# Second attention: VectorE scales each head's first two probability tiles, and the second head's first scores and the exchange stand inside the last value slab

## The chip, the core and the metric

The kernel runs on one core of one Trainium2 chip. Its engines work side by side, each through its own list of instructions, and meet at semaphores: TensorE (PE, matrix products into PSUM), VectorE (DVE), ScalarE (ACT), GpSimd (POOL), and SyncE (SP), which issues the transfers of the weights. The metric is the device time of one execution in microseconds (us), the median of several.

## The reference

Two blocks of two layers each over 512 tokens of width 1024, all in 32-bit floats. The first block has two layers of latent attention, a spatial gate, pooling windows and a gated feed-forward part. The second block has a short-convolution layer and a layer of dilated window attention, each with an MLP and a gated projection behind it. The change is in the dilated attention alone. What is computed there:

```python
q = partial_rotary(qkv[:, :, 0], positions)      # 3 groups x 8 heads of 128
k = partial_rotary(qkv[:, :, 1], positions)
v = qkv[:, :, 2]
for g, (window, dilation) in enumerate(((128, 1), (512, 4), (2048, 16))):
    s = einsum(q, k) * 128 ** -0.5               # band of at most 128 keys back
    lse = logsumexp(s)
    probs = exp(s - lse)
    o_g, lse_g = probs @ v, lse
weights = softmax(stack(lses), axis=0)           # over the three groups
o = sum(weights * outs)                          # one output per head
```

For one head this is one softmax over all three groups' scores, so each probability tile is multiplied in the end by one factor per row (the reciprocal of the mass of all groups).

## The kernel before

**The stages.** All weights come as a stream of slabs of 128 x 2048 numbers. SyncE loads a slab into one of two places, GpSimd splits it into a high and a low part (w_high, L449, by tensor_scalar, and w_low, L454, by tensor_tensor, four pieces each), and TensorE multiplies three times per block (L568 to L570: high by high, low by high, high by low) with the activations, which are split alike. A slab takes TensorE 48 matmuls. The heavy loops are all of this kind.

**The second attention** (`attn` on each engine) runs in two batches of four heads. A batch is twelve slabs for queries and keys, six for values (`for g in range(GROUPS): for half in range(2)`), then the four heads, with one more slab behind the first batch and the output projection of four slabs behind the second. Ahead of the last value slab, (g, half) = (2, 1), TensorE makes all scores of the batch's first head H0. A value slab's second half ends in four quarters, c = 0 to 3, one PSUM bank (4 + c) each, and ScalarE evicts each quarter to v_tok (L1495), which counts drained[4 + c].

**A head** has eight score tiles, 0 to 7 (128x256 each, tile 4 is 128x128), in four pairs, one PSUM bank a pair. Tiles 0 to 3 hold the dilated groups, 4 to 7 the near one. In steps, with the names of the code:

- `scores(H, k)`, TensorE: pair k (L979 for pairs 0 and 1, L985 for 2 and 3).
- `mask_tile(H, n)`, VectorE, L2003: adds the mask, writes the tile to `probs`, and takes the row's extreme. `exponential(H, n)`, ScalarE, L1465: the exponential in place, with the row's sum.
- `send(H, set_)`, VectorE, L2010: lays out these statistics. `exchange(H)`, TensorE, L996: moves them between rows, since the groups order their tokens differently, into a free corner of PSUM bank 2.
- `difference(H)` and `make_factors(H)`, VectorE, L2017 to L2027, with ScalarE's `stats_exponential(H)`, L1470, between them: the factors of the head, `factors_made`.
- `scale_head(H)`, GpSimd, L522: all eight tiles times their factors, in order, `tile_scaled` counted for each.
- `turn_pair(H, k)`, TensorE, L1008: transposes pair k of the scaled tiles, when they are scaled. `copy_turned(H, k)`: the transposed pair to SBUF, pairs 0 and 2 by ScalarE (L1477), 1 and 3 by VectorE (L2034).
- `values_pair(H, k)`, TensorE, L1026: product with the values. `copy_out(H)`, VectorE, L2039: the head's output.

Everything is in the order in which it is written, engine by engine; there is no scheduler. TensorE interleaves two heads: scores of H + 1 between the transposes and values of H, and the last two value pairs of H - 1 before scores pair 2 of H + 1. In the fourth head of a batch, the slab behind the batch fills the time until the factors. GpSimd does between the scalings, in the first batch, pieces of the split of the slab that comes two later (`pieces`, L504 and L511), and in the second batch the split of finished heads' outputs (`split_head`, L529 and L531), and behind the eighth head all pieces of the output projection's second slab. The outputs of heads 6 and 7 are split by ScalarE (L1254) and VectorE (L2088).

Of the kernel before, what the change touches and what calls it, by code (L numbers as in the profile page):

```python
# [175 lines left out]
def build(nc, a):  # L176

    ctx = ExitStack()
    with ctx:
# [3 lines left out]
        def sem(name):  # L183
            return ctx.enter_context(nc.semaphore(name))
# [164 lines left out]
        tile_scaled = sem("tile_scaled")  # L349
        pair_turned = sem("pair_turned")  # L350
# [90 lines left out]
        def _(pool):  # L441
# [73 lines left out]
            def scale_head(H):  # L515

                pool.wait_ge(factors_made, H + 1)
                for n in range(TILES):
                    at, w = tile_columns(n)
                    a, set_ = tile_slot(n)  # L520
                    tile = probs[:, H % 2, at:at + w]
                    pool.tensor_scalar(tile, tile, fac[:, H % 2, 3, a, set_:set_ + 1], None, ALU.mult).then_inc(tile_scaled, 1)  # L522
# [42 lines left out]
        def _(pe):  # L565
# [433 lines left out]
            def turn_pair(H, k):  # L999

                pe.wait_ge(tile_scaled, TILES * H + 2 * k + 2)
                if k >= 2:
                    pe.wait_ge(pair_copied[k - 2], H + 1)
                else:
                    at_least(pe, pair_copied[k + 2], H)
                for n in range((PAIR_AT[k + 1] - PAIR_AT[k]) // P):
                    at = PAIR_AT[k] + n * P
                    last = pe.transpose(ps[:, 4 + k % 2, n * P:(n + 1) * P], probs[:, H % 2, at:at + P], ident[:])  # L1008
                last.then_inc(pair_turned, 1)
# [21 lines left out]
            def attn(p):  # L1031
# [27 lines left out]
                for batch in range(2):  # L1059
# [18 lines left out]
                    for g in range(GROUPS):  # L1078
                        for half in range(2):
# [8 lines left out]
                            for c in range(TOK):  # L1088
                                if half == 0:
# [18 lines left out]
                    for b in range(4, 8):  # L1108
                        if b >= 6:
                            pe.wait_ge(drained[b], p.drain[b] + used[b])  # L1110
                    for j in range(BATCH_HEADS):
                        H = H0 + j
                        if j < BATCH_HEADS - 1:
                            scores(H + 1, 0)
                            exchange(H)
# [10 lines left out]
                            turn_pair(H, 1)  # L1126
                            values_pair(H, 0)
# [50 lines left out]
        def _(act):  # L1178
# [272 lines left out]
            def attn(p):  # L1451
# [27 lines left out]
                for batch in range(2):  # L1479
# [4 lines left out]
                    for g in range(GROUPS):  # L1484
# [3 lines left out]
                        for c in range(TOK):  # L1488
                            act.wait_ge(*((tile_done, t0 + 3 * g + c + 1) if c < 3 else (slab_done, s0 + 2 * g + 2)))
# [6 lines left out]
                    for j in range(BATCH_HEADS):  # L1496
                        H = H0 + j
                        stats_exponential(H)
# [51 lines left out]
        def _(dve):  # L1550
# [408 lines left out]
            def attn(p):  # L1959
# [60 lines left out]
                def make_factors(H):  # L2020
# [6 lines left out]
                    dve.reciprocal(fac[:, H % 2, 3], mass).then_inc(factors_made, 1)  # L2027

# [237 lines left out]
```

## Time and profile before

| what | value |
|---|---|
| median of 3 runs | 2636.18 us (2635.54 to 2640.35) |
| profiled execution | 2643.82 us, span 2641.8 us |
| TensorE (PE) busy | 2571.2 us, 97% of the span |
| GpSimd (POOL) busy | 1824.0 us, 69% |
| VectorE (DVE) busy | 1081.3 us, 41% |
| ScalarE (ACT) busy | 472.8 us, 18% |
| granted TensorE clock, mean | 0.987 |
| scaling of tiles, L522, 64 of them | 55.5 us |

The profiled execution has a span, from its first to its last instruction, and a time, which also holds what lies around it (2.0 us here). "Busy" is the sum of an engine's instructions. A row of the order of time shows the start, the time and the number of like instructions in a row, and in brackets how long the engine had idled before it and what ended that. TensorE's matmuls overlap, so a matmul of 0.40 us may be followed by the next after 0.23 us. The two batches' heads run from about 1889 to 1922 us and from about 2130 to 2165 us.

### The profile page before, as it was taken

To read this page: it belongs to the slowest core of one execution; us is meant where nothing else is said; L and a number is where in the kernel's file an instruction comes from. 1 tells how busy PE (TensorE), PEld (TensorE's weight loads), DVE (VectorE), ACT (ScalarE), POOL (GpSimd) and SP (SyncE) were. 2 spreads that over 40 slices of the span, in tenths; PEclk is the share of its full clock that TensorE was granted. 3 is DMA by queue.
4 is the path that set the end of the run, shared out by engine and by line. 5 is a ranking of instruction groups with operands and counts; after the bars stand their busy time and mean duration, and the time that the engine had idled before them with its cause. 6 is when DMAs were issued, how large, how long until landed. Compare 5 with 4: busy or idle time off the path is not lost.

```text
span 2641.8 us, 31829 instructions
## 1 busy us (share of the span) xinstructions
PE 2571.2 (97%) x11758; PEld 2133.6 (81%) x11758; DVE 1081.3 (41%) x1706; ACT 472.8 (18%) x886; POOL 1824.0 (69%) x1837
## 2 busy tenths in 40 slices
PE   7989999999899999999999999999999989999997
PEld 6768888888688888888888888888888978888885
DVE  4763332036633330344530422795378244504225
ACT  3432111023421110200200102300300032100022
POOL 5537777665267777677786776787677777867763
PEclk9999999999999999999999999999999999999998
DMA  4112222231122222222322222222112203222221
GB/s 155 49 48 95 96 95 96 95 118 49 38 106 95 95 95 96 96 96 96 104 96 96 95 97 98 97 96 97 63 64 95 99 30 104 96 96 96 96 97 63
DMA packets 36895, 236.46 MB, mean 90 GB/s; under 512 B 4048, under 2 KB 5584, under 8 KB 9168
## 3 DMA queue, kind: packets, MB, share of 16 engines
q1 hardware_dynamic: 33456, 230.78, 25.2%
q10 hardware_dynamic: 3360, 4.57, 0.6%
q8 instruction: 56, 0.92, 0.1%
q14 instruction: 23, 0.19, 0.0%
HBM read 233.24 MB, written 2.10 MB: 89 GB/s over the span
## 4 chain that ended last, share of the span: by engine, by line
PE 92%; DVE 3%; POOL 2%; issue 2%; ACT 1%; DMA 0%; DVEq 0%; SPq 0%; POOLq 0%; ACTq 0%
PE psum L568 29%; PE psum L569 29%; PE psum L570 29%; POOL probs L522 2%; PE psum L788 1%; PE psum L902 1%; POOL w_low L454 1%; PE psum L918 0%; PE psum L598 0%; DMA x_res<-in_x 0%; PE psum L1026 0%; PE psum L934 0%; PE psum L615 0%; POOL w_high L449 0%; PE psum L862 0%
## 5 line engine op out<-in xcount | busy, mean ns | idle before, releaser
L454 POOL TENSOR_TENSOR w_low<-w_stage,w_high 128x512 fp32r<-128x512 f32 x856 | 1145.4, 1370 | 17.9
L449 POOL TENSOR_SCALAR w_high<-w_stage 128x512 fp32r<-128x512 f32 x856 | 567.3, 690 | 731.8 <-PE psum L570 720.3
L568 PE MATMUL psum<-x_high,w_high 128*128 128x512 f32 x1664 | 655.7, 394 | 15.9 <-DVE x_low L1581 15.0
L569 PE MATMUL psum<-x_low,w_high 128*128 128x512 f32 x1664 | 649.4, 390 | 0.0
L570 PE MATMUL psum<-x_high,w_low 128*128 128x512 f32 x1664 | 649.0, 390 | 0.0
L568 PEld LDWEIGHTS psum<-x_high,w_high 128*128 128x128 f32 x1664 | 313.4, 188 | 84.3 <-issue 17.4
L569 PEld LDWEIGHTS psum<-x_low,w_high 128*128 128x128 f32 x1664 | 313.5, 188 | 67.3 <-issue 2.4
L570 PEld LDWEIGHTS psum<-x_high,w_low 128*128 128x128 f32 x1664 | 313.4, 188 | 65.4
L1618 DVE TENSOR_TENSOR psum<-psum,x_res 128x512 f32<-128x512 f32 x64 | 44.8, 700 | 465.4 <-PE psum L570 462.5
L568 PE MATMUL psum<-mlp_high,w_high 128*128 (+1 forms) x576 | 224.1, 389 | 0.0
L569 PE MATMUL psum<-mlp_low,w_high 128*128 (+1 forms) x576 | 224.1, 389 | 0.0
L570 PE MATMUL psum<-mlp_high,w_low 128*128 (+1 forms) x576 | 224.1, 389 | 0.0
L568 PE MATMUL psum<-attn_x_high,w_high 128*128 128x512 f32 x384 | 150.1, 391 | 0.0
L570 PE MATMUL psum<-attn_x_high,w_low 128*128 128x512 f32 x384 | 149.4, 389 | 0.0
L569 PE MATMUL psum<-attn_x_low,w_high 128*128 128x512 f32 x384 | 149.4, 389 | 0.0
L568 PE MATMUL psum<-ffn_high,w_high 128*128 (+1 forms) x352 | 136.9, 389 | 0.0
L569 PE MATMUL psum<-ffn_low,w_high 128*128 (+1 forms) x352 | 136.9, 389 | 0.0
L570 PE MATMUL psum<-ffn_high,w_low 128*128 (+1 forms) x352 | 136.9, 389 | 0.0
L1233 ACT ACTIVATE x_res<-psum 128x512 f32<-128x512 f32 x72 | 43.2, 600 | 493.9 <-DVE psum L1618 487.9
L568 PEld LDWEIGHTS psum<-mlp_high,w_high 128*128 128x128 f32 x576 | 108.1, 188 | 22.6
L570 PEld LDWEIGHTS psum<-mlp_high,w_low 128*128 128x128 f32 x576 | 108.1, 188 | 22.4
L569 PEld LDWEIGHTS psum<-mlp_low,w_high 128*128 128x128 f32 x576 | 108.1, 188 | 22.3
(289 smaller groups left out, 3399.8 us busy)
## 6 DMA issues: line engine op xcount, KB each, us to landing
w_stage<-in_wstream SPq DMA_DIRECT2D x216, 1024.0 KB, 4.9
x_res<-in_x SPq DMA_DIRECT2D x2, 1024.0 KB, 11.8
out_x<-attn_out SPq DMA_DIRECT2D x8, 256.0 KB, 2.1
inv_count_sb<-in_inv_count ACTq DMA_DIRECT2D x2, 512.0 KB, 8.8
ple_proj<-in_p ACTq DMA_DIRECT2D x2, 512.0 KB, 3.6
w_spat<-in_spatial ACTq DMA_DIRECT2D x2, 256.0 KB, 5.2
diag_sb<-in_diag ACTq DMA_DIRECT2D x2, 256.0 KB, 9.4
qk<-in_mask ACTq DMA_DIRECT2D x1, 306.0 KB, 2.9
```

Source lines behind the costliest of these rows:

```text
L449: last = pool.tensor_scalar(wh[:, s, part], stage[:, s, part], 1.0, 1.0, ALU.mult, ALU.mult)
L454: last = pool.tensor_tensor(wl[:, s, part], stage[:, s, part], wh[:, s, part].bitcast(F32), ALU.subtract)
L522: pool.tensor_scalar(tile, tile, fac[:, H % 2, 3, a, set_:set_ + 1], None, ALU.mult).then_inc(tile_scaled, 1)
L568: pe.matmul(out, wa, ra, start=start, stop=False)
L569: pe.matmul(out, wa, rb, start=False, stop=False)
L570: return pe.matmul(out, wb, ra, start=False, stop=stop)
L788: last = pe.matmul(ps[:, 6, at + c:at + c + 1], W[rows, n % 2, c * P:(c + 1) * P], ones[rows, 0:1], start=True, stop=True)
L902: last = pe.matmul(ps[:, h % 2, kb * P:], vt1[:, kb, h * V_HEAD:(h + 1) * V_HEAD], pt1[:, kb, kb * P:], start=kb == 0, stop=kb == TOK - 1)
L1233: act.activation(x[:, m, :], ps[:, m, :], ACT.Copy)
L1618: tt(ps[:, m, :], ps[:, m, :], x[:, m, :], ALU.add).then_inc(x_summed, 1)
```

## The change

Three things are edited, in this attention alone.

1. VectorE scales tiles 0 and 1 of each head, in `make_factors`, right behind the factors, and counts `front_scaled`. GpSimd's `scale_head` starts at tile 2. `turn_pair(H, 0)` waits for `front_scaled`, the others for `tile_scaled` with six tiles a head.
2. TensorE makes scores pair 0 of the batch's second head and the exchange of the first head ahead of quarter c = 3 of the last value slab, and no more behind the slab. On ScalarE, `stats_exponential(H0)` stands ahead of the eviction of that quarter.
3. The wait for the evictions of banks 6 and 7 (`drained`) goes from behind the slab to the place ahead of `values_pair(H0, 0)`.

```diff
             def scale_head(H):
                 pool.wait_ge(factors_made, H + 1)
-                for n in range(TILES):
+                for n in range(2, TILES):
...
             def turn_pair(H, k):
-                pe.wait_ge(tile_scaled, TILES * H + 2 * k + 2)
+                if k == 0:
+                    pe.wait_ge(front_scaled, 2 * (H + 1))
+                else:
+                    pe.wait_ge(tile_scaled, (TILES - 2) * H + 2 * k)
...
                             for c in range(TOK):
+                                if (g, half, c) == (2, 1, 3):
+                                    scores(H0 + 1, 0)
+                                    exchange(H0)
...
-                    for b in range(4, 8):
-                        if b >= 6:
-                            pe.wait_ge(drained[b], p.drain[b] + used[b])
                     for j in range(BATCH_HEADS):
                         H = H0 + j
                         if j < BATCH_HEADS - 1:
-                            scores(H + 1, 0)
-                            exchange(H)
+                            if j:
+                                scores(H + 1, 0)
+                                exchange(H)
                             scores(H + 1, 1)
...
                             turn_pair(H, 1)
+                            if j == 0:
+                                for b in (6, 7):
+                                    pe.wait_ge(drained[b], p.drain[b] + used[b])
                             values_pair(H, 0)
...
                         for c in range(TOK):
+                            if (g, c) == (2, 3):
+                                stats_exponential(H0)
...
-                        stats_exponential(H)
+                        if j:
+                            stats_exponential(H)
...
                     dve.reciprocal(fac[:, H % 2, 3], mass).then_inc(factors_made, 1)
+                    dve.wait_ge(factors_made, H + 1)
+                    for n in range(2):
+                        tile = probs[:, H % 2, 2 * P * n:2 * P * (n + 1)]
+                        dve.tensor_scalar(tile, tile, fac[:, H % 2, 3, n, 0:1], None, ALU.mult).then_inc(front_scaled, 1)
```

TensorE at the end of the first batch's last value slab, before. The slab's last matmuls stand ahead; L979 and L985 are scores of the second head, L996 the exchange, L1008 the first head's transposes.

```order
L570 MATMUL psum<-w_high,attn_x_low 128x512
L979 MATMUL psum<-qk 128x128 [waits tile_masked,drained7,drained6]
L979 MATMUL psum<-qk 128x128 x3
L996 MATMUL psum<-sent_stats,turn 64x16 [waits stats_sent]
L996 MATMUL psum<-sent_stats,turn 64x16 x3
L979 MATMUL psum<-qk 128x128 [waits tile_masked]
L979 MATMUL psum<-qk 128x128 x3
L985 MATMUL psum<-qk 128x128 [waits stats_used,tile_masked]
L985 MATMUL psum<-qk 128x256
L1008 MATMUL psum<-ident,probs 128x128 [waits tile_scaled,drained5,drained4]
```

The same place in the changed kernel (L980, L986, L997 and L1012 are L979, L985, L996 and L1008 of before; between the exchange and the next scores stand the last quarter's twelve matmuls, of which the first and the last are shown).

```order
L571 MATMUL psum<-w_high,attn_x_low 128x512
L980 MATMUL psum<-qk 128x128 [waits tile_masked]
L980 MATMUL psum<-qk 128x128 x3
L997 MATMUL psum<-sent_stats,turn 64x16 [waits stats_sent]
L997 MATMUL psum<-sent_stats,turn 64x16 x3
L569 MATMUL psum<-w_high,attn_x_high 128x512
...
L571 MATMUL psum<-w_high,attn_x_low 128x512
L980 MATMUL psum<-qk 128x128 [waits tile_masked]
...
L986 MATMUL psum<-qk 128x128 [waits stats_used,tile_masked]
L986 MATMUL psum<-qk 128x256
L1012 MATMUL psum<-ident,probs 128x128 [waits front_scaled,drained5,drained4]
```

Scores pair 0 and the exchange now stand 12 matmuls ahead of the slab's end and wait for no eviction; the first transpose waits for VectorE's count in place of GpSimd's.

VectorE from the first head's difference to the second head's next masks, before (L2017 to L2027 make the factors, ISA L2003 is a mask):

```order
L2017 TENSOR_TENSOR factors<-own_stats,psum 128x8 [waits stats_turned]
L2018 TENSOR_SCALAR factors<-factors 128x8 [waits dve_step]
L2003 ISA probs,own_stats<-psum,mask 128x256
L2003 ISA own_stats 128x1
L2024 TENSOR_TENSOR factors<-factors,psum 128x8 [waits stats_exp]
L2026 TENSOR_TENSOR factors<-factors,own_stats 128x8 [waits stats_used]
L2027 RECIPROCAL factors<-factors 128x8 [waits dve_step]
L2003 ISA probs,own_stats<-psum,mask 128x256 [waits pair_scored]
```

And in the changed kernel (L2028 to L2038 make the factors, ISA L2014 is a mask):

```order
L2028 TENSOR_TENSOR factors<-own_stats,psum 128x8 [waits stats_turned]
L2029 TENSOR_SCALAR factors<-factors 128x8 [waits dve_step]
L2014 ISA probs,own_stats<-psum,mask 128x256
L2014 ISA own_stats 128x1
L2035 TENSOR_TENSOR factors<-factors,psum 128x8 [waits stats_exp]
L2037 TENSOR_TENSOR factors<-factors,own_stats 128x8 [waits stats_used]
L2038 RECIPROCAL factors<-factors 128x8 [waits dve_step]
L2042 TENSOR_SCALAR probs<-probs,factors 128x256 [waits factors_made]
L2042 TENSOR_SCALAR probs<-probs,factors 128x256
L2014 ISA probs,own_stats<-psum,mask 128x256 [waits pair_scored]
```

Two scalings stand ahead of the masks of tiles 2 and 3, in every head.

## Rows read from the trace of the kernel before

**Rows 1.** The page: busy time of the engines; chain that ended last, by line.

```profile
PE 2571.2 (97%) x11758; PEld 2133.6 (81%) x11758; DVE 1081.3 (41%) x1706; ACT 472.8 (18%) x886; POOL 1824.0 (69%) x1837
...
PE psum L568 29%; PE psum L569 29%; PE psum L570 29%; POOL probs L522 2%; PE psum L788 1%; PE psum L902 1%; POOL w_low L454 1%; PE psum L918 0%; PE psum L598 0%; DMA x_res<-in_x 0%; PE psum L1026 0%; PE psum L934 0%; PE psum L615 0%; POOL w_high L449 0%; PE psum L862 0%
```

**Rows 2.** Windows: stretch, length, busy us (instructions) of PE, PEld, DVE, ACT, POOL, clock, DMA.

```profile
1885.00:1922.50 37.50, 33.08 (x253) 28.47 (x252) 17.72 (x77) 17.04 (x59) 28.10 (x32) 1.00 0.02 8
2126.00:2165.50 39.50, 33.41 (x255) 28.76 (x254) 18.91 (x77) 17.06 (x59) 30.15 (x34) 1.00 0.03 10
2177.00:2185.00 8.00, 6.75 (x29) 4.95 (x29) 5.19 (x6) 2.40 (x5) 7.92 (x8) 1.00 0.00 0
```

**Rows 3.** Order of time, GpSimd: start, us, what, [idle before, what ended it].

```profile
1891.94 6.92 POOL L522 TENSOR_SCALAR probs<-probs,factors 128x256 f32<-128x256 f32 x8 [10.63 <-DVE factors L2027]
...
1902.21 6.95 POOL L522 TENSOR_SCALAR probs<-probs,factors 128x256 f32<-128x256 f32 x8 [1.01 <-DVE factors L2027]
...
2133.20 6.92 POOL L522 TENSOR_SCALAR probs<-probs,factors 128x256 f32<-128x256 f32 x8 [10.62 <-DVE factors L2027]
...
2144.38 6.96 POOL L522 TENSOR_SCALAR probs<-probs,factors 128x256 f32<-128x256 f32 x8 [0.36 <-DVE factors L2027]
```

**Rows 4.** Waits of 1885 to 1922.5, then 2126 to 2186: us, times, longest.

```profile
PE psum L1008 <- POOL probs L522: 3.4, 7, 1.5
...
PE psum L1008 <- POOL probs L522: 5.0, 8, 1.6
```

**Rows 5.** Order of time, TensorE, first batch's heads.

```profile
1889.05 1.13 PE L979 MATMUL psum<-qk 128*128 128x128 f32 x8 [0.82 <-issue]
...
1893.92 0.63 PE L1008 MATMUL psum<-ident,probs 128*128 128x128 f32 x4 [1.48 <-POOL probs L522]
...
1900.39 0.42 PE L996 MATMUL psum<-sent_stats,turn 128*64 128x16 f32 x8
...
1904.10 0.66 PE L1008 MATMUL psum<-ident,probs 128*128 128x128 f32 x4
...
1905.90 0.66 PE L1008 MATMUL psum<-ident,probs 128*128 128x128 f32 x4 [0.28 <-POOL probs L522]
...
1909.22 0.66 PE L1008 MATMUL psum<-ident,probs 128*128 128x128 f32 x4 [0.38 <-POOL probs L522]
```

**Rows 6.** Order of time, ScalarE's last evictions of the value slab; VectorE's reciprocal.

```profile
1885.45 0.69 ACT L1495 ACTIVATE v_tok_wide<-psum,stat 128x512 f32<-128x512 f32 x1 [2.13 <-PE psum L570]
1888.27 0.69 ACT L1495 ACTIVATE v_tok_wide<-psum,stat 128x512 f32<-128x512 f32 x1 [2.13 <-PE psum L570]
...
1891.63 0.20 DVE L2027 RECIPROCAL factors<-factors 128x8 f32<-128x8 f32 x1
```

**Rows 7.** Order of time, first block: VectorE's tile scaling twice, GpSimd's split.

```profile
147.33 0.35 DVE L1943 TENSOR_SCALAR work<-work,stat 128x256 f32<-128x256 f32 x1
...
133.10 1.28 DVE L1943 TENSOR_SCALAR work<-work,stat 128x256 f32<-128x256 f32 x1 [0.24 <-DVE stat L1942]
...
130.51 5.00 POOL L454 TENSOR_TENSOR w_low<-w_stage,w_high 128x512 fp32r<-128x512 f32 x4
```

**Rows 8.** Order of time, VectorE, factors of the second batch's second head.

```profile
2143.15 0.89 DVE L2026 TENSOR_TENSOR factors<-factors,own_stats 128x8 f32<-128x8 f32 x1
```

**Rows 9.** Order of time behind the last head: GpSimd, VectorE, TensorE.

```profile
2178.24 5.79 POOL L511 TENSOR_TENSOR w_low<-w_stage,w_high 128x512 fp32r<-128x512 f32 x4
...
2177.74 2.65 DVE L2088 TENSOR_TENSOR attn_low<-attn_out,attn_high 128x512 fp32r<-128x512 f32 x2
...
2178.74 0.50 PE L568 MATMUL psum<-attn_high,w_high 128*128 128x512 f32 x1 [0.26 <-DVE attn_low L2088]
...
2184.13 0.47 PE L568 MATMUL psum<-attn_high,w_high 128*128 128x512 f32 x1 [0.98 <-issue]
```

**Rows 10.** Order of time, TensorE, from the first head's scores to the slab.

```profile
1876.59 0.60 PE L568 MATMUL psum<-w_high,attn_x_high 128*128 128x512 f32 x1
1877.02 0.40 PE L569 MATMUL psum<-w_low,attn_x_high 128*128 128x512 f32 x1
```

More of the change, by code:

```diff
@@ L349, in build @@
         tile_scaled = sem("tile_scaled")
+        front_scaled = sem("front_scaled")
         pair_turned = sem("pair_turned")
```

## The prediction

> **What bounds the kernel now.** I read the page first, then the busy time in three stretches, then GpSimd's scalings in order of time, then what TensorE waits for. On the page TensorE is busy 97% of the span, and its three product lines make 87% of the chain. The only other line above 1% there is GpSimd's scaling of probability tiles, L522, with 2%, some 53 us [rows 1]; eight heads at 6.9 us [rows 3] are 55 us, so every one of the eight scalings is on the chain. A gain has to come out of the few stretches where TensorE idles. In the first batch of four heads it is busy 33.08 of 37.50 us (4.42 idle), in the second 33.41 of 39.50 (6.09 idle), in the 8 us after the last head 6.75 of 8.00 (1.25 idle), all at a granted clock of 1.00 [rows 2]. Together that is 11.8 us, and no edit of this stage can give more.
>
> GpSimd's rows show a loop: it scales eight tiles, idles until the next factors, and scales again; in the first batch the period is 1902.21 - 1891.94 = 10.27 us [rows 3]. The waits say how much of it TensorE feels: the transposes of L1008 waited for L522 3.4 us in the first batch and 5.0 in the second [rows 4]. The other idle time is 0.82 us ahead of the first scores behind the value slab, at 1889.05, and the same in the second batch (two in all) [rows 5]: they wait for drained 6 and 7, and ScalarE's last eviction runs from 1888.27 to 1888.96 [rows 6]. Last, TensorE waits 0.98 us at 2184.13 for the low part of an output slab, which GpSimd finished at 2178.24 + 5.79 = 2184.03 [rows 9].
>
> **The change, part by part.** (a) *Scores pair 0 of the second head and the exchange go ahead of the last quarter of the value slab.* No work is added; the wait for drained 6 and 7 moves behind turn_pair(H, 1). Before, from the first score (1889.05) to the reciprocal's end (1891.63 + 0.20) it took 2.78 us [rows 5, 6]. After, scores and exchange take about 1.4 us of TensorE, then come the slab's last 12 matmuls, 2.8 us by the distance of ScalarE's last two evictions (1885.45 to 1888.27) [rows 6], then pairs 1 and 2 of the scores, about 2 us. The factors are made halfway through those 12 matmuls, so the first transpose comes some 3.4 us behind them, and two tiles need 2 x 0.87 = 1.7 us even on GpSimd (6.92 for eight) [rows 3]. So 2 x 0.82 us goes, and so does the largest wait for L522, 1.48 us at 1893.92 [rows 5], with its like in the second batch. Quarter 3's eviction now has two score pairs and two transposes ahead of its reader, over 3 us, and takes 0.69 [rows 6]. The exponential of the factors stands ahead of that eviction on ScalarE; it would hold it up only if the exchange were late, and the statistics that are exchanged come from scores made ahead of this slab.
>
> Price: TensorE switches once more between the four-byte matmuls and the slab's. After the first head's scores the slab's first matmul was followed after 1877.02 - 1876.59 = 0.43 us [rows 10], where 2.82 / 12 = 0.235 is the rule. I take 0.2 us for each batch, 0.4; bounds 0 (it merges with the switch behind the slab) and 0.8 (twice as much).
>
> (b) *Tiles 0 and 1 on VectorE, six on GpSimd.* GpSimd's scaling shrinks by 1.7 to about 5.2 us, and its loop to 10.27 - 1.7 = 8.6 us. TensorE's own work in a period is 10.27 less the waits of 0.28 at 1905.90 and 0.38 at 1909.22 [rows 5]: 9.6 us. The loop is then TensorE's, with 1.0 us to spare on GpSimd, and all of [rows 4], 3.4 + 5.0 = 8.4 us, can go.
>
> What do the two tiles cost on VectorE? The nearest row is L1943, the same form (128x256, SBUF to SBUF, a factor per partition): 0.35 us at 147.33 with GpSimd idle, 1.28 us at 133.10, within GpSimd's tensor_tensor of 130.51 to 135.51 [rows 7]. Both engines start on the same factors, GpSimd 0.11 us after the reciprocal (1891.83 to 1891.94) [rows 3, 6]; VectorE, which waits for its own result, should be no later. So the first tile likely gets through at once and the second may wait for one GpSimd tile. Bounds for both: 0.7 and 2.6 us; I take 1.6. What of it does TensorE see? The exchange of head 1 ended at 1900.39 + 0.42 = 1900.81, its first transpose started at 1904.10, 3.3 us later [rows 5]. The factors are there about 1.3 us after the exchange (GpSimd's start at 1902.21 less 0.1), so the front tiles at 2.9: hidden, with 0.4 us to spare. At 2.6 us they would be 0.6 us late. Behind the two tiles on VectorE stand the masks of tiles 2 and 3, the copy of the head before and the masks of 4 and 5, and behind those ScalarE's exponentials; VectorE idled there, since masks 6 and 7 come only with scores pair 3. At 1.6 us they stay covered, barely.
>
> (c) *GpSimd against VectorE in the second batch.* There GpSimd also splits two heads' outputs between scalings: 2144.38 - 0.36 - 2140.12 = 3.9 us [rows 3]. VectorE's L2026, a step of 8 elements like the reciprocal at 0.20, took 0.89 beside it [rows 6, 8], and the loop is some 11 us. After, GpSimd needs 5.2 + 3.9 = 9.1 us for a head and TensorE 9.6. In the second head GpSimd is free before the factors, for the first head lasts longer; in the third its split can still run into them. I leave 0.4 us of waiting there (bounds 0 and 2).
>
> The Trainium skill has a rule for this place ("SBUF — State Buffer", section Who interferes with whom): a VectorE `tensor_scalar` between SBUF operands can enter a 2-port mode, it and a GpSimd instruction then exclude each other whole, and issue order decides who blocks. The rows at 0.35 and 1.28 agree. By that rule the second tile waits a whole GpSimd tile in every head, the 1.6 us; without it both would take 0.7. The sum is the same by either, since both are hidden.
>
> (d) *The tail.* GpSimd reaches the late slab 1.7 us sooner, less some 0.3 for standing behind VectorE; that covers the 0.98 us. What is late next: the low part of head 6's output, for which TensorE already waits 0.26 us at 2178.74. VectorE starts it at 2177.74 [rows 9], and GpSimd, earlier by then, will be at tensor_tensor pieces of 1.25 us (four in 5.00) [rows 7], which can block it for longer. I take 0.3 us more (bounds 0 and 0.9).
>
> **Sum.** Removed: 8.4 + 2 x 0.82 + 0.98 = 11.0 us. Added: 0.4 + 0.4 + 0.3 = 1.1. Net 9.9 us, off the profiled span of 2641.8 (to 2631.9) and off that execution's time of 2643.82 alike. That execution is 7.6 us above the median of the runs; I take the stage to be the same in both and subtract from the median: 2636.18 - 9.9 = 2626.3. What stands behind the stage moves forward as a block, since TensorE sets its pace [rows 1].
>
> **Rivals.**
> *A partial gain.* Both front tiles are blocked (2.6 us), and in the second batch the factor steps before them too. The first transpose of heads 1 and 2 of each batch is then 0.6 to 1.0 us late. For it: 0.89 and 1.28 us where GpSimd was busy [rows 7, 8]. Against: GpSimd starts from idle. Price 4 x 0.8 = 3.2 us: gain 6.7, 2629.5.
> *No change.* VectorE and ScalarE close a loop as long as GpSimd's was: the masks of 2 and 3 behind the front tiles delay the exponentials, the copy of the first transpose and the next exchange, and the periods stay 10.3 and 11. Only the first heads and the tail gain, 2 x (0.82 + 1.5) + 0.98 - 1.1 = 4.5 us: 2631.7.
> *Slower.* One mechanism, at L2042 on VectorE: its two tiles take turns with GpSimd's so badly that the first transpose comes later than now. From that transpose to the end of the next exchange TensorE needs 9.6 - 3.3 = 6.3 us, so a period exceeds today's mean of 10.6 once the front tiles are ready over 4.3 us after the exchange, at 1.5 us for each tile; to eat the other 4.5 us as well, the four middle periods must each lose 1.1 us, at 2.05 us for each. That is two GpSimd tiles for each of VectorE's, and no row shows it. At 2.8 us for each, the loss is 4 x 2.6 - 4.5 = 5.9 us: 2642.1.
>
> **Chances.** Forecast 0.72, partial gain 0.16, no change 0.09, slower 0.03. A measurement of this kernel can tell 0.2%, 5.3 us, from no change; two thirds of the partial case lie above that. Faster by over 0.2%: 0.83; within: 0.14; slower: 0.03. Range: from 2623.0 (all 11.8 us, and 1.4 for the scatter of the runs, which spread over 4.8) to 2631.5 (the partial case, and part of no change).
>
> **What would show it.** Right, if in the new trace the transposes have no wait for GpSimd, heads follow each other in 9.6 to 9.8 us in both batches, GpSimd's scaling takes 5.2 to 5.5 us and starts inside the value slab for the first head, and nothing waits at the second output slab. VectorE's tiles at 0.35 and about 1.2 us would confirm (b); two of over 1.2 with a wait of TensorE on them are the partial case. A wait for copies of transposed tiles at a period of 10.3 is the third. Wrong altogether, if the granted clock falls in the stage, or if time goes outside 1885 to 2185 us.

## The result, and the profile after

| | before | after |
|---|---|---|
| median of 6 runs each | 2636.42 us (2635.54 to 2640.35) | 2623.05 us (2617.34 to 2629.31) |
| ratio, with its 95% interval | | 0.9944, 0.9933 to 0.9955 |
| profiled execution, span | 2643.82, 2641.8 us | 2629.31, 2627.4 us |
| mean granted clock of that execution | 0.987 | 0.987 |

The change gains 14.8 us by the ratio and 14.5 between the two profiled executions. The two medians differ by 13.4. The forecast was 9.9, below the 11.9 to 17.7 us of the interval. Of the 2636.18 us from which it subtracted, the ratio leaves 2621.4 us, which lies below the range of 2623.0 to 2631.5 (the bare median of 2623.05 stands on its edge). The direction was right and the size was not.

The lines of the kernel after are numbered a little higher: L980 and L986 are scores, L997 the exchange, L1012 transposes, L1030 values, L523 GpSimd's scaling, L2042 VectorE's two tiles, L2038 the reciprocal, L569 to L571 the products. First the page of after, with the lines that answer to [rows 1]:

```profile
PE 2567.9 (98%) x11758; PEld 2135.2 (81%) x11758; DVE 1085.6 (41%) x1722; ACT 471.8 (18%) x886; POOL 1808.0 (69%) x1821
...
PE 96%; DVE 2%; ACT 1%; issue 1%; POOL 0%; DMA 0%; DVEq 0%; SPq 0%; POOLq 0%; ACTq 0%
```

GpSimd's scaling was 2% of the chain before; GpSimd as a whole is 0% of it now. Look also at TensorE's sum: 2571.2 us before, 2567.9 after, for the same 11758 matmuls, in two executions of the same mean clock. TensorE's instructions were not changed, only their order, so a sum that becomes 3.3 us shorter is where the surplus shows first. Next the windows of after, the two batches and the first 8 us of the tail (columns as in [rows 2]):

```profile
1885.00:1922.50 37.50, 37.31 (x280) 34.03 (x279) 21.93 (x91) 16.92 (x60) 26.81 (x31) 1.00 0.12 45
2117.00:2155.00 38.00, 37.76 (x280) 34.90 (x280) 22.29 (x91) 17.38 (x61) 26.36 (x30) 1.00 0.08 29
2165.00:2173.00 8.00, 8.00 (x35) 6.20 (x34) 4.32 (x5) 3.36 (x6) 7.39 (x8) 1.00 0.25 75
```

TensorE idles 0.2 us a batch where it idled 4.4 and 6.1 [rows 2], at the same clock of 1.00. Now the order of time, TensorE, first batch of after: the scores and the exchange inside the slab, the slab's end, and then one head, to be held against [rows 5]:

```profile
1886.04 1.05 PE L980 MATMUL psum<-qk 128*128 128x128 f32 x8
1887.02 0.42 PE L997 MATMUL psum<-sent_stats,turn 128*64 128x16 f32 x8
1887.37 0.62 PE L569 MATMUL psum<-w_high,attn_x_high 128*128 128x512 f32 x1
1887.83 0.40 PE L570 MATMUL psum<-w_low,attn_x_high 128*128 128x512 f32 x1
...
1890.18 0.40 PE L571 MATMUL psum<-w_high,attn_x_low 128*128 128x512 f32 x1
1890.41 1.05 PE L980 MATMUL psum<-qk 128*128 128x128 f32 x8
...
1891.96 0.60 PE L1012 MATMUL psum<-ident,probs 128*128 128x128 f32 x4
...
1896.83 1.06 PE L980 MATMUL psum<-qk 128*128 128x128 f32 x8
...
1905.85 0.50 PE L980 MATMUL psum<-qk 128*128 128x128 f32 x3
```

No bracket is left. GpSimd (answers to [rows 3]), second head of the first batch and second and third of the second:

```profile
1899.63 5.26 POOL L523 TENSOR_SCALAR probs<-probs,factors 128x256 f32<-128x256 f32 x6 [3.18 <-DVE factors L2038]
...
2134.83 5.25 POOL L523 TENSOR_SCALAR probs<-probs,factors 128x256 f32<-128x256 f32 x6 [1.65 <-DVE factors L2038]
...
2144.38 5.30 POOL L523 TENSOR_SCALAR probs<-probs,factors 128x256 f32<-128x256 f32 x6 [0.37 <-DVE factors L2038]
```

GpSimd waits for the factors now and nobody waits for it. VectorE, the factors and the two tiles of two of these heads (answers to [rows 6] and [rows 8]):

```profile
1899.33 0.20 DVE L2038 RECIPROCAL factors<-factors 128x8 f32<-128x8 f32 x1
1899.57 0.84 DVE L2042 TENSOR_SCALAR probs<-probs,factors 128x256 f32<-128x256 f32 x2
...
2143.34 0.69 DVE L2037 TENSOR_TENSOR factors<-factors,own_stats 128x8 f32<-128x8 f32 x1
2144.07 0.20 DVE L2038 RECIPROCAL factors<-factors 128x8 f32<-128x8 f32 x1
2144.31 0.84 DVE L2042 TENSOR_SCALAR probs<-probs,factors 128x256 f32<-128x256 f32 x2
```

Both tiles together take 0.84 us. L2037 took 0.69 us in the second of these heads, where it takes 0.17 in the others. Last the tail, GpSimd, VectorE and TensorE at the second output slab (answers to [rows 9]):

```profile
2163.70 5.99 POOL L512 TENSOR_TENSOR w_low<-w_stage,w_high 128x512 fp32r<-128x512 f32 x4
...
2164.91 2.38 DVE L2103 TENSOR_TENSOR attn_low<-attn_out,attn_high 128x512 fp32r<-128x512 f32 x2
...
2169.86 0.39 PE L569 MATMUL psum<-attn_high,w_high 128*128 128x512 f32 x1
```

**Where the 14.4 us of the span went.** A column of idle time hides something here, so I count from start to start of TensorE's own rows. The stations of a batch are the first head's last scores, the scores pair 0 of heads 2, 3 and 4, and the fourth head's exchange. In the kernel after, the first row counts the slab without the scores and the exchange inside it, (1886.04 - 1876.05) + (1890.41 - 1887.37) = 13.03. The 1.33 us of those, 1887.37 - 1886.04, count with the head behind.

| stretch | first batch, before, after | gain | second batch, before, after | gain |
|---|---|---|---|---|
| value slab, to the scores behind it | 13.80, 13.03 | 0.77 | 13.80, 13.03 | 0.77 |
| to scores pair 0 of head 3 | 10.36, 7.75 | 2.61 | 10.36, 7.74 | 2.62 |
| to scores pair 0 of head 4 | 10.30, 9.02 | 1.28 | 11.21, 9.02 | 2.19 |
| to the exchange of head 4 | 12.46, 11.06 | 1.40 | 13.24, 11.21 | 2.03 |
| sum | 46.92, 40.86 | 6.06 | 48.61, 41.00 | 7.61 |

From the first matmul of the first output slab to the first of the second: 18.66 and 17.26, a gain of 1.40. All else, unchanged code: 0.8 us lost ahead of the first batch and 0.13 gained behind the tail. 6.06 + 7.61 + 1.40 + 0.13 - 0.8 = 14.4.

**The theories.** The head is what I went for: 10.30 us with 0.66 us of idle time [rows 5], and 9.02 after, with none.
A: a wait of TensorE costs more than the idle time that the trace shows at it, since a wait also breaks the overlap of neighbouring matmuls, and that part is booked as busy.
B: the surplus is the granted clock (runs of one kernel spread over some 10 us).
C: TensorE's own work in a head is 9.6 us as predicted, and the surplus was gained by something else, such as the move inside the slab.

### The profile page after: what moved, and what is told of

It is laid out like the page before. It is cut to its first block, busy times and chain, and to the rows that moved or that the text cites. A ratio compares the mean times of both kernels' runs of the same rounds, so it can differ in the third digit from the quotient of the medians.

```text
span 2627.4 us, 31829 instructions
## 1 busy us (share of the span) xinstructions
PE 2567.9 (98%) x11758; PEld 2135.2 (81%) x11758; DVE 1085.6 (41%) x1722; ACT 471.8 (18%) x886; POOL 1808.0 (69%) x1821
## 4 chain that ended last, share of the span: by engine, by line
PE 96%; DVE 2%; ACT 1%; issue 1%; POOL 0%; DMA 0%; DVEq 0%; SPq 0%; POOLq 0%; ACTq 0%
PE psum L569 30%; PE psum L570 30%; PE psum L571 30%; PE psum L1030 1%; PE psum L789 1%; PE psum L903 1%; PE psum L980 1%; PE psum L919 0%; PE psum L986 0%; PE psum L1012 0%; PE psum L599 0%; DMA x_res<-in_x 0%; PE psum L616 0%; PE psum L935 0%; PE psum L863 0%
## 5 line engine op out<-in xcount | busy, mean ns | idle before, releaser
L569 PE MATMUL psum<-x_high,w_high 128*128 128x512 f32 x1664 | 655.9, 394 | 15.6 <-DVE x_low L1592 15.0
L571 PE MATMUL psum<-x_high,w_low 128*128 128x512 f32 x1664 | 649.3, 390 | 0.0
L569 PEld LDWEIGHTS psum<-x_high,w_high 128*128 128x128 f32 x1664 | 313.7, 189 | 83.8 <-issue 17.4
L571 PEld LDWEIGHTS psum<-x_high,w_low 128*128 128x128 f32 x1664 | 313.5, 188 | 65.6
L569 PE MATMUL psum<-mlp_high,w_high 128*128 (+1 forms) x576 | 224.1, 389 | 0.0
L571 PE MATMUL psum<-mlp_high,w_low 128*128 (+1 forms) x576 | 224.1, 389 | 0.0
L569 PE MATMUL psum<-attn_x_high,w_high 128*128 128x512 f32 x384 | 150.1, 391 | 0.0
L571 PE MATMUL psum<-attn_x_high,w_low 128*128 128x512 f32 x384 | 149.4, 389 | 0.0
L569 PE MATMUL psum<-ffn_high,w_high 128*128 (+1 forms) x352 | 136.9, 389 | 0.0
L571 PE MATMUL psum<-ffn_high,w_low 128*128 (+1 forms) x352 | 136.9, 389 | 0.0
L571 PEld LDWEIGHTS psum<-mlp_high,w_low 128*128 128x128 f32 x576 | 108.1, 188 | 22.6
L569 PEld LDWEIGHTS psum<-mlp_high,w_high 128*128 128x128 f32 x576 | 108.1, 188 | 22.3
```

The lines of the kernel that those rows point to most:

```text
L569: pe.matmul(out, wa, ra, start=start, stop=False)
L571: return pe.matmul(out, wb, ra, start=False, stop=stop)
```

## The experiments

All runs below have their own runs of the kernel before beside them: 20, median 2637.47 us, for the first four; 10, median 2638.31, for the last four. "Stretch" means the sum rows of the table, first and second batch, and "period" scores pair 0 of head 3 to that of head 4. Diffs are against the changed kernel.

### The changed kernel once more

No edit.

> The changed kernel once more, unaltered, for the size of the gain and the granted clock of each run. In the two profiles the stretch from the first head's L985 scores to the slab behind the four heads went from 47.27 to 41.20 us (first batch) and from 48.96 to 41.35 (second), and the tail to the second output slab from 18.66 to 17.26: 6.07 + 7.61 + 1.40 = 15.1 us. Theory A (the surplus over the forecast 9.9 lies in waits that the idle column shows too small): the stretches repeat within 0.2 us, and the ratio is 0.9943 to 0.9950 (15.1 to 13.2 us). Theory B (part of the surplus is the clock, granted higher in the runs of the changed kernel): the ratio comes back to 0.996 with equal clocks, 10 us.

Measured: 2622.68 us median of 5, ratio 0.9944 (0.9929 to 0.9959). Stretches 40.86 and 41.55 us, period 9.02. The ratio and the first batch repeat to the last digit. The second batch is 0.55 us longer than in the first profile, outside the 0.2 us that was expected. Its rows show why: one of the steps that make the factors, eight numbers per row and 0.17 us long elsewhere, ran beside a piece of GpSimd's split and ended with it (order of time, VectorE and GpSimd).

```profile
2140.32 1.29 DVE L2029 TENSOR_SCALAR factors<-factors 128x8 f32<-128x8 f32 x1
...
2140.32 1.27 POOL L532 TENSOR_TENSOR attn_low<-attn_out,attn_high 128x512 fp32r<-128x512 f32 x1
```

### The scaling alone

The move is undone: scores pair 0 and the exchange stand behind the slab again, the wait for the evictions ahead of them, and `stats_exponential(H0)` on ScalarE at its old place (not shown).

```diff
                             for c in range(TOK):
-                                if (g, half, c) == (2, 1, 3):
-                                    scores(H0 + 1, 0)
-                                    exchange(H0)
...
+                    for b in (6, 7):
+                        pe.wait_ge(drained[b], p.drain[b] + used[b])
                     for j in range(BATCH_HEADS):
                         H = H0 + j
                         if j < BATCH_HEADS - 1:
-                            if j:
-                                scores(H + 1, 0)
-                                exchange(H)
+                            scores(H + 1, 0)
+                            exchange(H)
```

> VectorE scales tiles 0 and 1, but scores and exchange stay behind the value slab, as before. Theory A: heads 1 and 2 have the period of 9.02 us of the changed kernel in both batches; the first head keeps the 0.82 us wait for the eviction and a short wait for the front tiles (factors + 0.84 us against the end of scores pair 2, about 0.3 us), so each batch loses 1.3 to 1.6 us against the changed kernel: stretches of 42.6 and 42.8 us, 2.8 us in all, gain about 12 us. Theory C (TensorE's own work is 9.6 us a head, as the idle column has it, and the rest comes with the earlier exchange and the copies behind it): period 9.6, gain 9 us.

Measured: 2626.22 us median of 10, ratio 0.9960 (0.9948 to 0.9972). Stretches 42.57 and 43.53. The windows of one period in each batch:

```profile
1897.91:1906.93 9.02, 9.02 (x79) 8.46 (x78) 6.55 (x28) 5.23 (x19) 8.01 (x11) 1.00 0.00 1
2134.82:2144.32 9.50, 9.40 (x79) 8.44 (x78) 7.40 (x28) 5.00 (x19) 8.97 (x11) 1.00 0.01 2
```

The period of the first batch is 9.02 without the move, so TensorE's own work in a head is at most 9.0 us, and C, as far as it puts the surplus down to the move, falls. (That it did not come from the early front tiles is for the padded runs below.) The second batch missed the expectation: a stretch of 43.53 where 42.8 was expected, and a period of 9.50. There GpSimd has almost no time to spare. From one scaling to the next it takes 2148.03 - 2138.52 = 9.51 us, as long as the period: 5.2 for six tiles, 3.9 for two outputs, and 0.37 until the factors. The factors are late because a step of theirs is held up by the last piece of GpSimd's own split, and ends with it, as in the run before (order of time, VectorE and GpSimd):

```profile
2137.30 0.88 DVE L2029 TENSOR_TENSOR factors<-factors,own_stats 128x8 f32<-128x8 f32 x1
...
2136.89 1.27 POOL L532 TENSOR_TENSOR attn_low<-attn_out,attn_high 128x512 fp32r<-128x512 f32 x1
```

The idle column shows 0.10 of the 0.48 us; the weight loads (PEld) waited 0.21, 0.23 and 0.29 us in that period, for VectorE's tiles, ScalarE's copy and GpSimd. The order of time, TensorE, shows what the move is for:

```profile
1889.22 1.13 PE L980 MATMUL psum<-qk 128*128 128x128 f32 x8 [0.82 <-issue]
...
1893.02 0.63 PE L1012 MATMUL psum<-ident,probs 128*128 128x128 f32 x4 [0.41 <-DVE probs L2034]
```

Without it the first head's first transposes wait for VectorE's tiles.

### The move alone

GpSimd scales all eight tiles again, VectorE none.

```diff
-                for n in range(2, TILES):
+                for n in range(TILES):
...
-                    for n in range(2):
-                        tile = probs[:, H % 2, 2 * P * n:2 * P * (n + 1)]
-                        dve.tensor_scalar(tile, tile, fac[:, H % 2, 3, n, 0:1], None, ALU.mult).then_inc(front_scaled, 1)
```

> Scores and exchange move into the value slab, GpSimd scales all eight tiles, as before. Theory A: GpSimd closes the loop again, periods of heads 1 and 2 at 10.3 and 11.2 us as before, tail as before (18.7), while the first head gains all its four waits with their hidden part, 3.4 us a batch: stretches 43.9 and 45.6, gain 6.8 us in all. By the idle column alone the first head would gain 0.82 + 1.48 + 0.22 + 0.36 - 0.2 = 2.7 us a batch, 5.4 in all.

Measured: 2629.69 us median of 9, ratio 0.9967 (0.9955 to 0.9978). Stretches 43.22 and 44.65, shorter than theory A expected by 0.7 and 0.95 us; the second batch's period is 10.86, not 11.2. The windows of one period, then TensorE in the first of them:

```profile
1895.78:1906.07 10.29, 9.63 (x79) 8.34 (x78) 6.05 (x26) 5.22 (x19) 9.04 (x12) 1.00 0.00 1
2133.41:2144.27 10.86, 9.65 (x79) 8.33 (x78) 6.53 (x26) 5.23 (x19) 10.41 (x12) 1.00 0.01 2
```

```profile
1902.27 0.66 PE L1009 MATMUL psum<-ident,probs 128*128 128x128 f32 x4 [0.28 <-POOL probs L523]
...
1905.58 0.66 PE L1009 MATMUL psum<-ident,probs 128*128 128x128 f32 x4 [0.38 <-POOL probs L523]
```

With the old scaling the first batch's period, its 9.63 us of busy time and both waits are those of before. The halves overlap: in the first batch the scaling alone gains 4.35 us, the move alone 3.70, and both 6.06, not 8.05. The 2.0 us that both claim lie in the first head, up to the scores pair 0 of head 3: there the scaling alone gains 1.67 us, the move alone 2.91, and both 2.61. Its largest wait for scaled tiles is 1.48 us by its bracket in [rows 5].

### The scaling made long again, first try

Everything as changed, but GpSimd multiplies two tiles by 1.0 ahead of its six, so that it should be late as before while VectorE still has its two tiles.

```diff
                 pool.wait_ge(factors_made, H + 1)
+                for n in (6, 7):
+                    at, w = tile_columns(n)
+                    tile = probs[:, H % 2, at:at + w]
+                    pool.tensor_scalar(tile, tile, 1.0, 1.0, ALU.mult, ALU.mult).then_inc(padded, 1)
                 for n in range(2, TILES):
+                    if n == 6:
+                        pool.wait_ge(padded, 2 * (H + 1))
...
```

> The changed kernel with two more GpSimd instructions (tiles 6 and 7 times 1.0) ahead of its six scalings, so that VectorE still makes the front tiles early, while GpSimd's part takes 7.0 us as before. Theory A (each wait of a transpose costs its idle time and an exposed weight load and pipeline start): the period goes back to 10.3 us in the first batch and 11.2 in the second, with only 0.3 to 0.4 us of idle time shown at the second and fourth transpose; gain as with the move alone, 6.8 us. Theory C (the surplus of 0.6 us a head came from the early front tiles): period 9.7 and 10.6.

Measured: 2623.41 us median of 4, ratio 0.9946 (0.9928 to 0.9964). Stretches 41.46 and 42.62, period 9.39. I had mis-sized the pad: the two took 0.96 us, not 1.85, since a tile times two immediate numbers takes 0.5 us where one times a factor per row takes 0.92. So neither theory's figure for the period (10.3 and 9.7) applies. Still, the period grew by 0.37 us and TensorE's rows show a wait of 0.15.

### The same with a longer pad

Four tiles, 4 to 7, instead of two.

> As the padded kernel before it, but with four idle GpSimd instructions (tiles 4 to 7 times 1.0): two took 0.96 us there, not the 1.85 wanted. GpSimd's part of a head is then 1.92 + 5.1 = 7.0 us, as in the kernel before, with the front tiles on VectorE. Theory A (a wait of a transpose costs its idle time and some 0.2 us of exposed weight load and pipeline start): periods back to 10.2 to 10.4 us in the first batch and 11.0 to 11.3 in the second, the stretch from the first head's L985 scores to the fourth exchange 43.2 to 43.6 us in the first batch (40.86 in the changed kernel) and 44.5 to 45.2 in the second, while the idle column shows no more than 0.7 us a head. Theory C (the early front tiles give the surplus): periods 9.7 and 10.6.

Measured: 2627.78 us median of 5, ratio 0.9962 (0.9949 to 0.9976). Stretches 42.56 and 44.59, periods 9.91 and 11.04. GpSimd and TensorE in the first batch, order of time, and the window of that period:

```profile
1898.55 1.47 POOL L523 TENSOR_SCALAR probs<-probs 128x128 f32<-128x128 f32 x4 [1.42 <-DVE factors L2045]
1900.00 5.12 POOL L530 TENSOR_SCALAR probs<-probs,factors 128x256 f32<-128x256 f32 x6
```

```profile
1905.18 0.66 PE L1019 MATMUL psum<-ident,probs 128*128 128x128 f32 x4 [0.36 <-POOL probs L530]
```

```profile
1895.76:1905.67 9.91, 9.43 (x79) 8.42 (x78) 6.93 (x28) 5.23 (x19) 8.49 (x14) 1.00 0.01 2
```

The pad was short again (1.47 us; pad and six tiles are 6.59, eight tiles were 6.92), and the first batch fell short of what A expected: a period of 9.91 for 10.2 to 10.4, a stretch of 42.56 for 43.2 to 43.6. The second batch's 11.04 and 44.59 lie in A's ranges. By its size alone the first batch's period, between C's 9.7 and A's 10.2, would decide nothing. The comparison inside the period does not depend on the pad's length: it grew by 9.91 - 9.02 = 0.89 us, of which TensorE's idle time is 0.48 and its "busy" time 9.43 - 9.02 = 0.41; by C it would have grown by the idle time alone. VectorE, which the pad could have held up, did not cost it: its two tiles took 0.89 us, and the first transposes came 1900.31 - 1899.65 = 0.66 us behind their scores, as in after. That is A, on its own.

### GpSimd held until VectorE's tiles are done

```diff
             def scale_head(H):

-                pool.wait_ge(factors_made, H + 1)
+                pool.wait_ge(front_scaled, 2 * (H + 1))
```

> GpSimd's scale_head waits for front_scaled in place of factors_made, so that it starts when VectorE has done its two tiles. If the two engines exclude each other, VectorE's pair takes 0.6 us (2 x 0.27 to 0.35, pipelined) in place of 0.84; if its 0.84 us is VectorE's own time, it stays 0.84. GpSimd starts 0.5 to 0.8 us later after the factors; with 1.0 to 1.3 us to spare in the first batch the stretch there stays at 40.9 us within 0.2; in the second batch, where GpSimd has no slack, up to 1 us more.

Measured, a single run, so no gain is read from its time: 2619.09 us at a mean clock of 0.991. Stretches 41.18 and 41.81, periods 9.34 and 9.20. The first batch is 0.08 us outside what was expected. VectorE's two tiles, GpSimd held:

```profile
1896.90 0.62 DVE L2042 TENSOR_SCALAR probs<-probs,factors 128x256 f32<-128x256 f32 x2
```

0.62 us against 0.84 with GpSimd at work, and GpSimd's six take 5.10 instead of 5.26. So the two engines do get in each other's way here, for 0.22 us a head on VectorE. Avoiding it starts GpSimd some 0.7 us later, and the first batch's period is 0.3 us longer. TensorE does not wait for GpSimd there but for VectorE's copy of the second pair (L2049, 0.24 us by its bracket): the `send` ahead of that copy took 0.51 us in this period, where after has 0.19.

### The wait for the evictions ahead of the scores again

The move stays; only its third part is undone.

```diff
+                    for b in (6, 7):
+                        pe.wait_ge(drained[b], p.drain[b] + used[b])
                     for j in range(BATCH_HEADS):
...
-                            if j == 0:
-                                for b in (6, 7):
-                                    pe.wait_ge(drained[b], p.drain[b] + used[b])
                             values_pair(H, 0)
```

> The changed kernel with the wait for drained 6 and 7 back behind the value slab, ahead of scores pair 1 of the second head. TensorE then waits for ScalarE's eviction of the last quarter, 0.8 us of idle time as before, and by theory A 0.2 us that the idle column does not show: both stretches 1.0 us longer (41.9 and 42.0 to 42.5), 2 us in all. By the idle column alone 0.8 us each.

Measured: 2624.31 us median of 4, ratio 0.9951 (0.9936 to 0.9966). Stretches 42.04 and 42.39, periods 9.03 and 9.02. TensorE at the slab's end:

```profile
1883.06 0.40 PE L571 MATMUL psum<-w_high,attn_x_low 128*128 128x512 f32 x1
1884.29 1.13 PE L980 MATMUL psum<-qk 128*128 128x128 f32 x8 [0.82 <-issue]
```

From start to start 1.23 us, where after has 1890.41 - 1890.18 = 0.23. The wait costs 1.00 us at its place, and its bracket says 0.82; the first batch's stretch is 1.18 us longer than with the wait moved. This is the second time that an added wait costs more than its idle time, at another line and with another releaser. (The remaining 0.18 us of the 1.18 lies behind this place.)

### The copy of the second pair ahead of the statistics

The changed kernel still has short waits of the weight loads for VectorE's copies. In the waits of 1885 to 1918 us of after:

```profile
PEld psum L1030 <- DVE probs_t L2049: 0.9, 4, 0.3
```

This version copies the second pair first, and spreads GpSimd's splits of the second batch otherwise.

```diff
-                        for h in ((0, 1), (2, 3), (4,), (5,))[j]:
+                        for h in ((0, 1), (2,), (3, 4), (5,))[j]:
...
-                            send(H + 1, 0)
                             copy_turned(H, 1)
+                            send(H + 1, 0)
```

> A try at a faster version: VectorE copies the second transposed pair ahead of its send (in the changed kernel TensorE's weight loads of L1030 wait 0.15 to 0.3 us a head for that copy), and GpSimd splits one output less before the third head of the second batch, where its split runs into VectorE's factors (0.16 and 0.55 us of wait in two profiles), and one more behind it. First-batch stretch 40.86 less 0.1 to 0.5 us, second batch 41.0 to 41.5 down to 40.6; 0.5 to 1.2 us in all, less than the time of a run can tell, so the ratio stays at 0.994 to 0.9945. The rival: the send comes later, the exchange of the next head with it, and nothing is gained.

Measured: 2621.72 us median of 5, ratio 0.9938 (0.9924 to 0.9951). Stretches 40.34 and 40.45 us, periods 8.92 in both. The stretches are the shortest of all, 0.52 and 0.55 below after. The first batch has the copy's edit alone, so its 0.52 us is the copy's; in the second batch the two edits are not separated. It also shows that the 9.02 us of after still held 0.1 us of waiting. In the time of a whole execution, 1 us is less than these runs can tell from the changed kernel (0.9933 to 0.9955).

## Why the prediction was right in direction and wrong in size

**The failed step** is one assumption with two faces: "TensorE's own work in a period is 10.27 less the waits of 0.28 [...] and 0.38 [...]: 9.6 us", and "Together that is 11.8 us, and no edit of this stage can give more". Both take the idle column for the whole cost of a wait. TensorE's own work in a period is at most 9.02 us, and the stage gave 15.07 us in its two stretches and the tail. The term of the sum that this mis-sized is the waits for GpSimd: 8.4 - 0.4 = 8.0 us predicted, 12.1 measured. Here is what the column leaves out. TensorE and its weight loads (PEld) in one head of after, order of time:

```profile
1900.72 0.82 PE L986 MATMUL psum<-qk 128*128 128x128 f32 x4
1901.38 0.60 PE L1012 MATMUL psum<-ident,probs 128*128 128x128 f32 x4
1901.81 1.03 PE L986 MATMUL psum<-qk 128*128 128x256 f32 x4
1902.68 0.60 PE L1012 MATMUL psum<-ident,probs 128*128 128x128 f32 x4
```

```profile
1901.16 0.57 PEld L1012 LDWEIGHTS psum<-ident,probs 128*128 128x128 f32 x4
...
1902.46 0.57 PEld L1012 LDWEIGHTS psum<-ident,probs 128*128 128x128 f32 x4
```

The same places before, where the transposes had to wait (their own rows are 1904.10 and 1905.90 in [rows 5]):

```profile
1903.30 0.82 PE L985 MATMUL psum<-qk 128*128 128x128 f32 x4
...
1904.59 1.03 PE L985 MATMUL psum<-qk 128*128 128x256 f32 x4
```

```profile
1904.10 0.42 PEld L1008 LDWEIGHTS psum<-ident,probs 128*128 128x128 f32 x4 [0.38 <-POOL probs L522]
...
1905.90 0.42 PEld L1008 LDWEIGHTS psum<-ident,probs 128*128 128x128 f32 x4 [0.68 <-POOL probs L522]
```

After, a transpose's weights are loaded 0.22 us ahead of it (1901.16, 1901.38) and it starts while the scores' modelled end still runs (1900.72 + 0.82 = 1901.54). Before, load and transpose start together. The tile that is waited for is the stationary operand, so its load does not go ahead; and the idle column begins to count only where the scores' modelled end runs out. The first transposes stood at 1904.10 with no bracket on PE at all, yet came 0.80 us behind their scores instead of 0.66; PEld's row tells it, 0.38. By start to start:

| from, to | before | after | more | shown idle |
|---|---|---|---|---|
| scores pair 2, first transposes | 0.80 | 0.66 | 0.14 | none |
| scores pair 3, second transposes | 1.31 | 0.87 | 0.44 | 0.28 |
| values pair 0, third transposes | 1.00 | 0.89 | 0.11 | none |
| values pair 1, fourth transposes | 1.43 | 1.00 | 0.43 | 0.38 |
| inside the four groups of transposes | 1.87 | 1.71 | 0.16 | none |

Together 1.28 us, and 0.66 shown. The windows of the same period say it in one line each, first before (1899.41, 2140.67), then after:

```profile
1899.41:1909.71 10.30, 9.64 (x80) 8.34 (x78) 6.05 (x26) 5.22 (x19) 9.29 (x13) 1.00 0.00 1
2140.67:2151.88 11.21, 9.67 (x79) 8.34 (x78) 6.71 (x26) 5.23 (x19) 10.68 (x13) 1.00 0.01 1
```

```profile
1896.83:1905.85 9.02, 9.02 (x80) 8.47 (x79) 6.55 (x28) 5.22 (x19) 6.22 (x7) 1.00 0.00 1
2132.02:2141.04 9.02, 9.02 (x79) 8.46 (x78) 6.55 (x28) 5.22 (x19) 7.29 (x9) 1.00 0.01 2
```

The same 79 or 80 matmuls are 9.64 us "busy" with waits between them and 9.02 without. A good part of this could have been had before the change. PEld's waits for GpSimd stand beside PE's, 4.6 us against 3.4 in the first batch and 6.1 against 5.0 in the second; that is 2.3 us more, and still less than what came. And in the eighth head of before, where nothing waits for GpSimd, the fourth transposes follow values pair 1 after 2174.55 - 2173.66 = 0.89 us, against 1.43 with a shown wait of 0.38.

**Theory B falls** by comparing runs at the same mean clock, in us:

| clock | before | after, again |
|---|---|---|
| 0.987 | 2643.6 (3 runs, median) | 2629.3 (the profiled one of after) |
| 0.989 | 2637.8 (median) | 2621.8 to 2622.8 |
| 0.990 | 2633.9 to 2635.8 | 2621.2 |

The gain is 14.3 us in the first line, 15.0 to 16.0 in the second and 12.7 to 14.6 in the third, so above 9.9 in each. The clock is given to 0.001, and a step of that is 2.6 us of 2630, so this says no more than that. The clock in the stage is 1.00 in every window; what spreads the runs lies ahead of it (the stage's first station stood at 1875.25, 1876.05 and 1873.69 us in before, after and after again, and at 1864.35 in the single run with GpSimd held, at 0.991). The surplus is in the two stretches and the tail, at a clock of 1.00.

**The terms one by one.**

- (a) *The move.* Predicted 2 x 0.82 less 2 x 0.2; measured 2 x 0.77. The switch came out right: 1887.83 - 1887.37 = 0.46 against a step of 0.23, so 0.23 us. It was the wait that was worth 1.00 each, not 0.82. That the first transposes come some 3.4 us behind the factors held, as 3.2: the reciprocal ended at 1888.74, they stand at 1891.96, and nobody waited.
- (b) *The front tiles.* Predicted 1.6 us, hidden; measured 0.84, hidden. The rule of the Trainium skill ("SBUF — State Buffer", section Who interferes with whom), by which one of the tiles would wait for a whole GpSimd tile, is not borne out here in its price: the single tiles take 0.35 to 0.57 us over the 16 of them, beside GpSimd tiles of 0.92. That the two hold each other up shows (0.84 us against 0.62 for VectorE's pair, 5.26 against 5.10 for GpSimd's six), but by far less than a tile; why, and in which mode VectorE ran, no run here shows. I had read 1.28 us off a case with GpSimd's tensor_tensor as neighbour [rows 7], and beside that instruction a whole one's wait does occur: 1.29 us for a step of 0.17 in the second run of the changed kernel. GpSimd's tile I took at 0.87 us, which is the mean of eight with one half tile among them; a whole one takes 0.92.
- (b) and (c) *The waits for GpSimd.* Predicted 8.4 - 0.4 = 8.0 us over both batches. Measured, all of the table but its first row: 5.29 + 6.84 = 12.1. This is the mis-sized term, by the mechanism above. The second batch's 0.4 us was about right. The stretch to the exchange of head 4 has 11.06 us in the first batch, and in the second, where GpSimd's split holds up a step of the factors, 11.21 in the first profile of the changed kernel and 11.77 in the next: 0.15 and 0.71 us.
- (d) *The tail.* Predicted 0.98 - 0.3; measured 1.40. GpSimd's pieces end at 2163.70 + 5.99 = 2169.69 and the slab starts at 2169.86, in step. The block on VectorE's L2103 did not come: 2.38 us against 2.65. The shown wait of 0.26 us at head 6's output, which was to grow by 0.3, is gone (from start to start 0.66 us before, 0.40 after). And the 0.98 us of idle time was worth more than it showed, as in the heads: from start to start 2184.13 - 2182.75 = 1.38 us before, 2169.86 - 2169.63 = 0.23 after.
- *The rivals.* None came. Partial gain and slower needed front tiles of 1.3 us each and more; no change needed a period of 10.3. ("Today's mean of 10.6" in the slower case is 10.7 by [rows 3], 10.27 and 11.18; nothing hangs on it.) What I had put down as what would confirm the forecast, "9.6 to 9.8 us" for a head, was itself the failed step, and 9.02 named it at once.

## What to carry to other kernels

In every wait measured here TensorE's idle column showed less than the wait cost. Where a matmul's stationary operand is late, measure from start to start against the same pair of lines at a place without a wait, and look at PEld's waits; here each wait that showed cost 0.1 to 0.2 us more than it showed, and two of the four in a head did not show at all. Two edits that attack the same wait do not add: here 4.35 and 3.70 us made 6.06.

## What the runs showed of the hardware

- A "busy" sum is not work: 79 to 80 matmuls were booked as 9.64, 9.43, or 9.02 us by how often TensorE had to wait between them.
- VectorE's two tiles of 128x256 took 0.84 us with GpSimd scaling beside them and 0.62 with GpSimd held, a difference of 0.22 us where one GpSimd tile takes 0.92. Beside GpSimd's tensor_tensor of 1.27 us, single VectorE steps of 0.17 us took up to 1.29 and ended with it.
- GpSimd's tensor_scalar in place on 128x256 took 0.92 us (median) with a factor per row, and 0.42 to 0.50 with two immediate numbers.
